# Rounding weight slabs in quarters inside the index stage of a hybrid decoder block

## The reference, cut to what matters

```
h = RMSNorm(x)                                    # x is 512 tokens x 1024
q_sb,k_sb,v_sb | q_sa,k_sa,v_sa | q_idx,k_idx,w_idx | g_sb,g_sa = split(h @ W_in)
rel   = q_idx . k_idx * 32**-0.5                  # 8 index heads, 32 wide
score = sum over heads of w_idx * relu(rel)       # causal; the best 128 keys of each query are kept
o_sa  = softmax attention with ALiBi over the kept keys
o_sb  = stick-breaking attention
x = x + (sigmoid(g_sb)*(o_sb@W_sb) + sigmoid(g_sa)*(o_sa@W_sa)) @ W_out
x = x + relu(RMSNorm(x) @ W1)**2 @ W2
```

## Time and profile before

| | |
|---|---|
| median of 3 runs | 757.88 us (757.83 to 757.93) |
| profiled execution | 757.77 us |
| its span | 755.7 us |
| PE busy | 733.2 us, 97% of the span |
| DVE busy | 525.5 us, 70% |
| ACT busy | 335.0 us, 44% |
| POOL busy | 223.6 us, 30% |

### The profile page before, as it was taken

The page is one execution under the profiler, slowest core; times in us unless marked ns, Lnnn a source line. Parts: engine busy times, 40 slices in busy tenths (PEclk is TensorE's granted clock), DMA queues, the critical chain, the costliest instruction groups (busy, mean ns, idle before and its releaser), DMA issues.

```text
span 755.7 us, 9738 instructions
## 1 busy us (share of the span) xinstructions
PE 733.2 (97%) x3482; PEld 579.6 (77%) x3482; DVE 525.5 (70%) x730; ACT 335.0 (44%) x477; POOL 223.6 (30%) x193
## 2 busy tenths in 40 slices
PE   8999999999999999899999999999999999999998
PEld 4768778777777555578887888888888888888886
DVE  5354786788996866545664568787786959595972
ACT  5234644256664666842233344443515253524320
POOL 2113424100001445102121036361709081625610
PEclk9999999999999999999999999999999999999999
DMA  9307322310111212113164133314060515131102
GB/s 329 124 15 200 135 73 94 112 56 1 56 56 56 56 57 56 56 56 112 56 208 154 57 112 104 119 56 169 4 213 4 167 55 167 56 111 56 56 15 98
DMA packets 43893, 70.63 MB, mean 93 GB/s; under 512 B 2641, under 2 KB 27217, under 8 KB 43858
## 3 DMA queue, kind: packets, MB, share of 16 engines
q1 hardware_dynamic: 43858, 70.17, 28.0%
HBM read 65.71 MB, written 2.10 MB: 90 GB/s over the span
## 4 chain that ended last, share of the span: by engine, by line
PE 88%; DVE 5%; ACT 3%; POOL 2%; issue 1%; DMA 0%; SPq 0%; DVEq 0%; ACTq 0%
PE ps L1692 7%; PE ps L1693 7%; PE ps L1694 7%; PE ps L415 6%; PE ps L417 6%; PE ps L416 6%; PE ps L1720 6%; PE ps L1721 6%; PE ps L1722 6%; PE ps L408 6%; PE ps L410 5%; PE ps L409 5%; PE ps L1541 2%; PE ps L1577 2%; PE ps L1618 1%; DVE cut_lo L399 1%
## 5 line engine op out<-in xcount | busy, mean ns | idle before, releaser
L1692 PE MATMUL ps<-b_hi,cut_hi 128*128 128x512 f32 (+1 forms) x272 | 102.6, 377 | 0.0
L1693 PE MATMUL ps<-b_lo,cut_hi 128*128 128x512 f32 (+1 forms) x272 | 102.4, 377 | 0.0
L1694 PE MATMUL ps<-b_hi,cut_lo 128*128 128x512 f32 (+1 forms) x272 | 102.4, 376 | 0.0
L415 PE MATMUL ps<-cut_hi,a_hi 128*128 128x512 f32 x224 | 90.0, 402 | 1.3 <-DVE a_lo L990 1.3
L417 PE MATMUL ps<-cut_hi,a_lo 128*128 128x512 f32 x224 | 87.6, 391 | 0.0
L416 PE MATMUL ps<-cut_lo,a_hi 128*128 128x512 f32 x224 | 87.4, 390 | 0.0
L399 DVE TENSOR_TENSOR cut_lo<-raw,cut_hi 128x2048 fp32r<-128x2048 f32 (+1 forms) x30 | 58.5, 1950 | 33.9 <-ACT cut_hi L391 33.8
L609 POOL TENSOR_TENSOR a_lo<-qo_sb,a_hi 128x512 fp32r<-128x512 f32 x49 | 78.2, 1620 | 5.6 <-ACT a_hi L868 5.6
L858 ACT ACTIVATE qo_sb<-ps 128x512 f32<-128x512 f32 x32 | 19.2, 599 | 136.5 <-PE ps L1694 91.9
L597 POOL TENSOR_SCALAR qo_sb<-qo_sb 128x128 f32<-128x128 f32 (+3 forms) x28 | 30.2, 1078 | 128.7 <-DVE snmax L1162 128.0
L391 ACT ACTIVATE cut_hi<-raw 128x2048 fp32r<-128x2048 f32 (+1 forms) x30 | 48.7, 1622 | 42.0 <-PE ps L410 23.4
(11 more groups left out here) (192 smaller groups left out, 1652.6 us busy)
## 6 DMA issues: line engine op xcount, KB each, us to landing
raw<-in_w_ff_dram SPq DMA_DIRECT2D x32, 1024.0 KB, 5.5
raw<-in_w_in_dram SPq DMA_DIRECT2D x16, 1024.0 KB, 5.2
gates<-in_x_dram SPq DMA_DIRECT2D x8, 512.0 KB, 5.7
raw<-in_w_out_dram SPq DMA_DIRECT2D x4, 1024.0 KB, 4.9
raw<-in_w_in_dram SPq DMA_DIRECT2D x4, 512.0 KB, 6.0
raw<-in_w_branch_sb_dram SPq DMA_DIRECT2D x2, 1024.0 KB, 5.0
raw<-in_w_branch_sa_dram SPq DMA_DIRECT2D x4, 512.0 KB, 6.1
out_dram<-gates SPq DMA_DIRECT2D x8, 256.0 KB, 2.0
```

The costliest lines, as they stand in the source:

```text
L415: nc.tensor.matmul(dst, l_hi, w_hi, start=start, stop=False)
L1692: T.matmul(dst, w_hi[:, w], b_hi[:, k, a:b], start=(k == 0), stop=False)
L1693: T.matmul(dst, w_hi[:, w], b_lo[:, k, a:b], start=False, stop=False)
L1694: mm = T.matmul(dst, w_lo[:, w], b_hi[:, k, a:b], start=False, stop=(k == KD - 1))
```

## The change

Three slabs are rounded at other places.

- **Slab 3, low part.** It was rounded by VectorE after the last block of KVI was scaled and before the four L1088 subtractions. Now two of these come first, then the slab, then the other two. The slab is still done in one piece.
- **Slab 5, low part.** It was done in one piece before part 0 of the scores. Now it is done in four pieces of 128 x 512, one after each of the scores 0 to 3.
- **Slab 6, high part.** It was done in one piece after the square of block 9. Now it is done in four pieces, one after each of the relus 16 to 19.
- **Slab 6, low part.** It was done in one piece after `head_scaled` 8 and before score 16. Now it is done in four pieces, one after each of the scores 20 to 23.

The order of the DMA queue, of GpSimd and of TensorE is as it was.

```
-            def index_relus(part):
+            def index_relus(part, cut=None):
...
                     A(rel[u % 2][:, 0:w], bank(6 + u % 2, 0, w), ACT.Relu, scale=IXD ** -0.5).then_inc(relu_done, 1)
+                    if cut is not None:
+                        act_cut(cut, u % 4, 4)
...
                         if g == KSB:
-                            index_relus(2 + m)
+                            index_relus(2 + m, 2 * g + 2 if m == 2 else None)
                         square(4 * g + m)
-                        if g == KSB and m == 1:
-                            act_cut(2 * g + 2)
...
-            def index_scores(part):
+            def index_scores(part, cut=None):
...
                                                op0=ALU.mult, op1=ALU.add).then_inc(score_done, 1)
+                    if cut is not None:
+                        dve_cut(cut, u % 4, 4)
...
                         V.tensor_tensor(q_parts[1][:, :, t], bank(4 + m % 2, P, 3 * P).rearrange("p (a b) -> p a b", a=2),
                                         q_parts[0][:, :, t].bitcast(F32), ALU.subtract).then_inc(tr_out, 1)
+                        if m == 1:
+                            dve_cut(2 * KVI + 3)
                 if g == KSB:
                     dve.wait_ge(w_ready, 1)
-                    index_scores(0)
+                    index_scores(0, 2 * QSB + 3)
                     index_scores(1)
...
                         for m in range(TB):
-                            index_scores(2 + m)
+                            index_scores(2 + m, 2 * g + 2 if m == 3 else None)
...
-                            if m == 1:
-                                dve_cut(2 * g + 2)
...
-                dve_cut(2 * g + 3)
+                if g not in (KVI, QSB):
+                    dve_cut(2 * g + 3)
```

## The result

The changed kernel took **760.28 us** (median of 7, 759.44 to 760.99) against 757.88; the ratio is 1.0032, with a 95% interval of 1.0023 to 1.0041. So it is slower by 2.4 us, 0.3%. The runs also lie further apart: 1.55 us between the fastest and the slowest, against 0.31 before. The profiled execution took 760.19 us, its span (first to last instruction) is 758.5.

The account below looks back on a forecast made before the run. TensorE, 88% of the chain, was taken as the bound, losing time only where it waits. Terms -0.93 - 1.14 + 2.8 = +0.7 us gave 758.5 profiled, median 758.6 us; range 757.8 to 761.2.

Parts of the forecast that it names:

- rival 1: The new TensorE stop before QSA lowers its clock: 1.9 us more, 760.5 us, at most 763.1; chance 0.33.
- Slab 3 and slab 5: TensorE's waits at the KVI turn and at logit 4 go away, gaining 0.93 and 1.14 us.
- Slab 6, the walk along VectorE and ScalarE: Slab 6's last quarter, after score 23, lands at 103.3 us; TensorE stops 4.4 to 5.5 us before QSA, losing 2.8.
- The base cost without the clock: Whole kernel, TensorE's clock unchanged: early gains and the loss at slab 6 sum to +0.7 us.
- the slower first matmul: At QSA's start after the stop: 0.1 us added for a slower first matmul.
- Quarters: VectorE's 128x512 pieces take 0.60 us each, 2.4 a slab against 2.2 whole; the skill's 150 cycles would cost 0.5 more.
- Nothing after 110 us: After 110 us nothing was foreseen to give or take time.

Follow-up runs that it names:

- kept_busy: The changed kernel plus 18 bf16 matmuls on zeros, result unread, on TensorE between logit 23 and the wait for slab 6: 758.02 us, ratio 1.0003.
- slab_3_only: The kernel before with only slab 3's low part moved as in the change: 756.85 us, ratio 0.9988.
- whole_after_23: The changed kernel with slab 6's low part in one piece after score 23, its high part still in quarters: 760.85 us, ratio 1.0043.

## Why the prediction was right or wrong

The time lies in the upper part of the range, and only because I had drawn the range to take in rival 1. The forecast I held likeliest, 758.6 and no measurable change, did not come. Rival 1 did, which I had given 0.33, with 760.5 us against 760.28 measured.

- **Slab 3 and slab 5**: right. -0.93 and -1.14 predicted, -0.89 and -1.05 measured alone, -2.05 together. Slab 3 followed the two subtractions at 52.17, and the third was not late (54.54).
- **Slab 6, the walk along VectorE and ScalarE**: right. The trace after is 2.18 us ahead at logit 16 (89.69). So score 20, predicted at 98.1, should be at 95.9 (it was at 95.97), a pair 1.28 long (1.27), and the last quarter down at 101.1 (101.11). The stop was 4.46 us by the profile, within the 4.4 to 5.5 given. QSA started 101.17 - 100.72 = 0.45 later than in the earlier trace rows, where the terms gave 0.7. Of the difference, 0.1 is the slower first matmul, which the 0.7 holds and a start doesn't, and 0.1 is that 2.18 us had been won by then and not 2.07.
- **The base cost without the clock**: +0.7 predicted, and right between the first and the last instruction. kept_busy has a span of 756.3 us against 755.7 (medians), and its first turn in QSA is at 104.05 against 103.45. Its time is only 0.2 above that of the kernel before, which can't be told from none. The missing 0.4 lies outside the instructions: time less span is 2.1 us before and 1.7 in the changed kernel. It is 1.7 in all runs that round a slab in quarters, and 2.1 in slab_3_only, the one changed kernel that rounds none so. The prediction had carried the 2.1 over; why it is less, no run shows.
- **The step that failed** is the weight given to rival 1: the sum has the clock at nothing, as if a stop of 5 us would probably leave it alone. I had no row of such a stop amid dense matmuls and put 0.33. All seven executions are at or above 759.4, and even a stop half as long cost the clock in seven executions of eleven. Its price was right: 1.9 predicted, 2.04 in the trace and 2.26 between medians. The wide spread of the changed kernel comes with it and is gone with kept_busy. That the low stretch isn't equally long in each execution is likely (the mean granted clock goes from 0.995 to 0.997), but the trace is of one of the seven only.
- **Quarters** at 0.60 from start to start cost 2.4 us against 2.2 in one piece, 0.07 for each further instruction, and between scores 20 to 23 they are no loss at all, as whole_after_23 shows. VectorE: DVE Perf Modes in the Trainium skill (section The TRN2 errata) has two figures for the fixed part of an operation. The 150 cycles that the prediction took, 0.16 us, again agree in kind only; the 58 cycles of its table, 0.06 us, are the size measured.
- **Nothing after 110 us** was predicted, and nothing was found that would explain microseconds. At the first turn in QSA TensorE is 106.08 - 103.45 = 2.63 us later than before, 0.45 from the start and 2.18 from the slow first block. At its last matmul it is 754.93 - 752.12 = 2.81 later, so some 0.2 came in between, at a place that I leave open. The spans differ by these 2.8, the times by 2.4, which is the 0.4 outside the instructions again.

## What to carry to other kernels

A piece of work that is cut up and pushed between others has its deadline where its last piece lies: ask first when its reader comes, and then count what stands before that piece on its engine. Here the same quarters four steps earlier turn 2.4 us lost into 3.6 us won (3.2 of them between the first and the last instruction). And a single stop of TensorE can cost more than its length. One stop of 4.5 us cost another 2 us afterwards, while four short waits that together lost about as much (4.3 by their starts) left the clock at full. If such a stop can't be avoided, useless matmuls in it are worth trying.

## What the runs showed of the hardware

- After 4.5 us without work TensorE's clock was at 0.50 in every execution of the changed kernel as far as their times tell. After 3.6 us it was so in seven of nine, and after 2.3 us in seven of eleven. I had not expected the shortest. Waits of up to 1.7 us, as one of 1.69 us at 314.7 us in the kernel before, left the granted clock at 1.00 in the stretches before and after.
- Seventeen recorded bf16 matmuls on zeros in the stop (18 in the program) held the clock in all eleven executions, as far as their times tell; with ten of them it fell in seven of eleven.
- The low clock doubles the distance between matmuls, 0.43 us instead of 0.23, and in the profiled execution it outlasted the stop by 105.60 - 101.17 = 4.4 us of dense matmuls.
